# Seven block products for eight in an input projection, with the block sums on GpSimd

## What is computed

```python
h = modulated rmsnorm of x                    # (2304, 1024)
parts = split(h @ w_in)                       # w_in (1024, 4096): q, k, v, gate of four head groups
A: window attention   B: neighbourhood attention   C: retention   D: HGRN2 (bounds from the forget columns)
mixed = concat(out_A * silu(gate_A), ..., out_D * silu(gate_D))
x = x + gate_mod * rmsnorm(mixed @ w_out)     # w_out (1024, 1024)
```

## Time and profile before

| | |
|---|---|
| time, median of 3 runs | 3869.07 us (3867.66 to 3869.54) |
| span of the profiled execution | 3870.5 us |
| TensorE busy | 3759.0 us, 97% |
| TensorE weight loads | 2057.6 us, 53% (beside matmuls) |
| VectorE, ScalarE, GpSimd busy | 2311.2, 1186.4, 515.0 us |
| HBM traffic | 386.67 MB, 100 GB/s |
| stages of layer 0 on TensorE | first 43 to 343 us, win to 767, nei to 1202, rest to 1560, HGRN and output to 1961 |

### The profile page before, as it was taken

One profiled execution on the slowest core, in us unless ns is written; L12 is line 12 of the kernel. 1 busy time (PEld: TensorE's weight loads), 2 busy tenths in 40 slices (PEclk: granted clock), 3 DMA queues, 4 the chain that ended last, 5 costly groups with the idle time before them and its releaser, 6 DMA issues.

```text
span 3870.5 us, 62967 instructions
## 1 busy us (share of the span) xinstructions
PE 3759.0 (97%) x24449; PEld 2057.6 (53%) x24449; DVE 2311.2 (60%) x4739; ACT 1186.4 (31%) x3257; POOL 515.0 (13%) x798
## 2 busy tenths in 40 slices
PE   7999999999999998899999999999999999989998
PEld 4544555545554455555544445554555545555554
DVE  2334345323667978999932333552246688889996
ACT  3311223223332122344442023222333311224443
POOL 2100000100000155100000000001000003540000
PEclk9999999999999999899999999999999999979999
DMA  7443121132222434332432031213222233352322
GB/s 249 139 140 103 50 72 53 61 105 69 88 88 86 130 104 129 134 124 99 145 120 90 38 102 50 69 48 115 70 82 73 74 119 115 117 165 96 123 100 85
DMA packets 234360, 388.87 MB, mean 100 GB/s; under 512 B 30001, under 2 KB 150033, under 8 KB 233937
## 3 DMA queue, kind: packets, MB, share of 16 engines
q1 hardware_dynamic: 194096, 262.55, 21.9%
q0 software_dynamic: 39968, 122.30, 8.3%
HBM read 264.42 MB, written 122.25 MB: 100 GB/s over the span
## 4 chain that ended last, share of the span: by engine, by line
PE 91%; DVE 5%; SPq 1%; DMA 1%; issue 1%; ACT 1%; POOL 0%; DVEq 0%; ACTq 0%; POOLq 0%
PE ps L1170 51%; PE ps L1524 13%; PE ps L1307 6%; PE ps L1289 4%; PE ps L1276 3%; PE ps L1280 2%; PE ps L1477 2%; PE ps L1439 2%; PE ps L1349 1%; PE ps L1236 1%; PE ps L1418 1%; PE ps L1502 1%; DVE e_t L2077 1%; PE ps L1182 1%; PE ps L1506 1%
## 5 line engine op out<-in xcount | busy, mean ns | idle before, releaser
L1170 PE MATMUL ps<-w_sb,hT 128*128 128x512 f32 x4608 | 2174.0, 606 | 3.7 <-ACT hT L1671 2.4
L1170 PEld LDWEIGHTS ps<-w_sb,hT 128*128 128x128 f32 x4608 | 812.5, 190 | 772.6 <-issue 737.8
L1524 PE MATMUL ps<-wo_sb,mT 128*128 128x512 f32 x1152 | 534.5, 604 | 2.6 <-ACT mT L1841 2.6
L979 POOL DMA_DIRECT2D projected<-row_t x252 | 137.1, 544 | 2336.5 <-DVE row_t L2080 1084.8
L2077 DVE RECIPROCAL e_t<-e_t 128x256 f32<-128x256 f32 (+1 forms) x180 | 430.7, 2393 | 6.2
L1524 PEld LDWEIGHTS ps<-wo_sb,mT 128*128 128x128 f32 x1152 | 205.9, 190 | 206.6 <-issue 196.5
L2075 DVE TENSOR_SCALAR e_t<-e_t 128x256 f32<-128x256 f32 (+1 forms) x180 | 62.2, 346 | 207.9 <-ACT row_t L1689 186.3
L1683 ACT ACTIVATE row_t<-ps 128x512 f32<-128x512 f32 x108 | 64.5, 597 | 393.9 <-PE ps L1170 388.0
L2184 DVE TENSOR_REDUCE nei_st<-ps 128x2 f32<-128x512 f32 x72 | 49.7, 691 | 211.1 <-PE ps L1280 211.1
L2217 DVE COPY win_pT<-ps 128x512 f32<-128x512 f32 x64 | 44.2, 691 | 213.5 <-PE ps L1289 213.5
L2217 DVE COPY nei_pT<-ps 128x512 f32<-128x512 f32 x64 | 44.2, 691 | 207.8 <-PE ps L1289 207.8
(11 more groups left out here) (248 smaller groups left out, 5172.5 us busy)
## 6 DMA issues: line engine op xcount, KB each, us to landing
projected<-row_t POOLq DMA_DIRECT2D x288, 256.0 KB, 2.5
w_sb<-in_w_in SPq DMA_DIRECT2D x14, 2048.0 KB, 9.2
hg_raw<-projected SPq DMA_DIRECT2D x72, 256.0 KB, 3.9
...
hg_braw<-projected SPq DMA_DIRECT2D x108, 128.0 KB, 2.6
...
```

The source lines that it names most:

```text
L979: pool.dma_start(rows[tok(t), g * GRP:(g + 1) * GRP], row_t[:, p.slot]).then_inc(row_stored[p.slot], 16)
L1170: mm = nc.tensor.matmul(ps[:, p.bank, :], hT[:, k, t * P:(t + 1) * P], w_sb[:, g % 2, k, :], start=(k == 0), stop=(k == KC - 1))
L1524: mm = nc.tensor.matmul(ps[:, 6 + g, :], mT[:, t % 2, k, :], wo_sb[:, k, g * GRP:(g + 1) * GRP], start=(k == 0), stop=(k == KC - 1))
```

## The change

For groups 0 to 5 two neighbouring tiles (t0 = 2i, t1 = 2i + 1) and one group make a *unit*: a block product of a 2x2 block matrix (tiles by halves of the inner channels) with a 2x2 block matrix (`b11`, `b12`, `b21`, `b22`: 512 channels x 256 columns each). It is computed by seven block products in the order P1, P2, P6, P5, P7, P3, P4, each of 4 matmuls of 128x256. Four of them have token sums as the stationary operand: s1 = t1 upper + t1 lower half, s3 = t0 upper - t1 upper, s2 = s1 - t0 upper, s4 = t0 lower - s2. Four have weight sums as the moving one: t2 = b22 - b12 + b11 (two operations), t1 = b22 - t2, t3 = t2 - b11, t4 = b21 - t2, made once for a group. All of these sums are GpSimd's: 4 of 128x512 for a unit, 5 of 128x1024 for a group. P6 and P7 accumulate in PSUM on P1, P3 on P5, P4 on P7.

ScalarE copies P1, P6, P5 and P4 out of PSUM (`take_part`), VectorE adds a kept part to P2, P7 and P3 on the way out (`add_part`); product k waits until product k - 2 of its bank is out. SiLU is made by 256-column blocks from `row_t` (`silu_block`). GpSimd's order for a unit is `unit_sums`: s4, the next unit's s1, at a change of group t2 and t1 of the next, s3, s2, then t3 and t4, then the two stores. The weights come in four block loads of 0.5 MB, issued by ScalarE while the last unit of the group before runs (after P1 the upper two, after P6 the lower two); layer 0's first by SyncE. `fill` gives 14 small matmuls to a slot (2, 3, 4, 2, 3), and still 8 large ones where pieces are plain. `LEAD` is one unit. In the first stage `turn_x` stands after 7 of a slot's 14 matmuls and `normed`, `modulated` run one tile further ahead. The 38 band DMAs stand behind the sums and stores of unit 1. At the end of layer 0 GpSimd makes layer 1's first sums. `oml` is gone and some tiles and semaphores share a place; groups 6 and 7 stay as they were.

```diff
-ALL_PIECES = ([(g, t) for g in range(6) for t in range(NT)] + [(g, BACK[i]) for g in (6, 7) for i in (0, 1)]
-              + [(g, t) for t in BACK[2:] for g in (6, 7)])
-
-LEAD = 2
+UNIT_GROUPS = 6
+PAIRS = NT // 2
+UNITS = [(g, i) for g in range(UNIT_GROUPS) for i in range(PAIRS)]
+PLAIN = ([(g, BACK[i]) for g in (6, 7) for i in (0, 1)] + [(g, t) for t in BACK[2:] for g in (6, 7)])
+LEAD = 1
 
...
-AT_WIN, AT_NEI, AT_REST = 2 * NT, 4 * NT + LEAD, 6 * NT + 2 * LEAD
-PROJ_ORDER = {"first": ALL_PIECES[:AT_WIN], "win": ALL_PIECES[AT_WIN:AT_NEI], "nei": ALL_PIECES[AT_NEI:AT_REST], "rest": ALL_PIECES[AT_REST:]}
+AT_WIN, AT_NEI = 2 * PAIRS, 4 * PAIRS + LEAD
+PLAIN_NEI = 2 * (NT + AT_NEI + LEAD - len(UNITS))
+UNIT_ORDER = {"first": UNITS[:AT_WIN], "win": UNITS[AT_WIN:AT_NEI], "nei": UNITS[AT_NEI:]}
+PLAIN_ORDER = {"first": [], "win": [], "nei": PLAIN[:PLAIN_NEI], "rest": PLAIN[PLAIN_NEI:]}
+P1, P2, P6, P5, P7, P3, P4 = range(7)
+BY_ACT = {P1: 1, P6: 2, P5: 3, P4: 4}
+BY_DVE = {P2: 1, P7: 2, P3: 3}
+S1, S3, S2, S4 = range(1, 5)
+HB = GRP // 2
+KH = KC // 2
+def w_places(g):
+    c, d, spare = ((2, 3, 7), (7, 2, 3), (3, 7, 2))[g % 3]
+    return {"b11": 0, "b21": 1, "b12": c, "t2": c, "b22": d, "t1": 4, "t3": 5, "t4": 6, "spare": spare}
+BLOCKS = {"b11": (0, 0), "b12": (0, 1), "b21": (1, 0), "b22": (1, 1)}
...
+    def load_block(eng, l, g, name):
+        kh, nh = BLOCKS[name]
+        at = g * GRP + nh * HB
+        src = w_in[l, kh * KH * P:(kh + 1) * KH * P, at:at + HB].rearrange("(k p) n -> p k n", p=P)
+        eng.dma_start(w_blk[:, w_places(g)[name], :].rearrange("p (k n) -> p k n", n=HB), src).then_inc(lower_in if kh else upper_in, 16)
...
+            def make_s1(u):
+                t0, t1 = u.tiles
+                if u.g == 0:
+                    pool.wait_ge(h_act, u.l * NT + t1 + 1)
+                    pool.wait_ge(h_dve, u.l * NT + t1 + 1)
+                nc.gpsimd.tensor_tensor(s_t[:, 0], half(t1, 0), half(t1, 1), ALU.add).then_inc(s_made, 1)
+            def make_s3(u):
+                t0, t1 = u.tiles
+                nc.gpsimd.tensor_tensor(s_t[:, 2], half(t0, 0), half(t1, 0), ALU.subtract).then_inc(s_made, 1)
+            def make_s2(u):
+                pool.wait_ge(s_made, 4 * u.u + S1)
+                nc.gpsimd.tensor_tensor(s_t[:, 1], s_t[:, 0], half(u.tiles[0], 0), ALU.subtract).then_inc(s_made, 1)
+            def make_s4(u):
+                pool.wait_ge(s_made, 4 * u.u + S2)
+                nc.gpsimd.tensor_tensor(s_t[:, 1], half(u.tiles[0], 1), s_t[:, 1], ALU.subtract).then_inc(s_made, 1)
+            def make_t2(d, g):
+                at, n, made = w_places(g), d * UNIT_GROUPS + g, 5 * (d * UNIT_GROUPS + g)
+                for half_in in (upper_in, lower_in):
+                    pool.wait_ge(half_in, 32 * (n + 1))
+                t2 = w_blk[:, at["t2"], :]
+                nc.gpsimd.tensor_tensor(t2, w_blk[:, at["b22"], :], t2, ALU.subtract).then_inc(t_made, 1)
+                pool.wait_ge(t_made, made + 1)
+                nc.gpsimd.tensor_tensor(t2, t2, w_blk[:, at["b11"], :], ALU.add).then_inc(t_made, 1)
+                pool.wait_ge(t_made, made + 2)
...
+            def store_unit(u):
+                for k, t in enumerate(u.tiles):
+                    p = u.rows[k]
+                    if k == 0:
+                        pool.wait_ge(part_dve, 3 * u.u + BY_DVE[P3])
+                    else:
+                        pool.wait_ge(part_act, 4 * u.u + BY_ACT[P4])
+                        pool.wait_ge(part_dve, 3 * u.u + BY_DVE[P7])
+                    last = [n for key, n in u.block.items() if key[0] == k]
+                    if last:
+                        pool.wait_ge(blk_silu, max(last) + 1)
+                    pool.dma_start(rows[tok(t), u.g * GRP:(u.g + 1) * GRP], row_t[:, p.slot]).then_inc(row_stored[p.slot], 16)
+            def unit_sums(g, i, between=None):
+                u = UNIT[l, g, i]
+                n = UNITS.index((g, i)) + 1
+                after = UNIT[(l,) + UNITS[n]] if n < len(UNITS) else None
+                turn = after is not None and after.g != g
+                pool.wait_ge(proj_done, u.run + P6 + 1)
+                make_s4(u)
+                if after is not None:
+                    pool.wait_ge(proj_done, u.run + P5 + 1)
+                    make_s1(after)
+                if between is not None:
+                    store_out(between)
+                if turn:
+                    make_t2(l, g + 1)
+                    make_t1(l, g + 1)
+                if after is not None:
+                    pool.wait_ge(proj_done, u.run + P7 + 1)
+                    make_s3(after)
+                    pool.wait_ge(proj_done, u.run + P3 + 1)
+                    make_s2(after)
+                if turn:
+                    make_t3(l, g + 1)
+                    pool.wait_ge(proj_done, u.run + P4 + 1)
+                    make_t4(l, g + 1)
+                store_unit(u)
+            if l == 0:
+                make_t2(0, 0)
+                make_t1(0, 0)
+                make_t3(0, 0)
+                make_t4(0, 0)
+                first = UNIT[l, 0, 0]
+                make_s1(first)
+                make_s3(first)
+                make_s2(first)
+            for n, (g, i) in enumerate(UNIT_ORDER["first"]):
+                unit_sums(g, i)
+                if l == 0 and n == (MAKE_AT + 19) // 2:
+                    pool.wait_ge(setup, SETUP_DVE + DEC_DVE)
                     pool.dma_start(decays, dec_new[:, :, :]).then_inc(tables_out, 16)
-                if l == 0 and n == 2:
+                if l == 0 and n == 1:
...
+                    def product(k, x, w, opens=False):
+                        if u.run + k >= 2:
+                            before = RUN[u.run + k - 2]
+                            if before[1] is None:
+                                bank_out(pe, before[0])
+                            else:
+                                part_out(pe, *before)
+                        for c in range(KH):
+                            mm = nc.tensor.matmul(ps[:, (u.run + k) % 2, 0:HB], x[:, c], w_blk[:, at[w], c * HB:(c + 1) * HB],
+                                                  start=opens and c == 0, stop=(c == KH - 1), skip_group_check=not opens)
+                            if c == KH - 1:
+                                mm.then_inc(proj_done, 1)
+                            yield
+                    def own(t, kh):
+                        return hT[:, kh * KH:(kh + 1) * KH, t * P:(t + 1) * P]
+                    new = i == 0
...
+                    yield from product(P1, own(t0, 0), "b11", opens=True)
+                    if new:
+                        pe.wait_ge(lower_in, 32 * (u.group + 1))
+                    yield from product(P2, own(t0, 1), "b21", opens=True)
+                    if new:
+                        pe.wait_ge(t_made, 5 * u.group + 2)
+                    pe.wait_ge(s_made, 4 * u.u + S2)
+                    yield from product(P6, s_t[:, 1], "t2")
+                    if new:
+                        pe.wait_ge(t_made, 5 * u.group + 3)
+                    pe.wait_ge(s_made, 4 * u.u + S1)
+                    yield from product(P5, s_t[:, 0], "t1", opens=True)
+                    if new:
+                        pe.wait_ge(t_made, 5 * u.group + 4)
+                    pe.wait_ge(s_made, 4 * u.u + S3)
+                    yield from product(P7, s_t[:, 2], "t3")
+                    pe.wait_ge(s_made, 4 * u.u + S4)
+                    yield from product(P3, s_t[:, 1], "b22")
+                    if new:
+                        pe.wait_ge(t_made, 5 * u.group + 5)
+                    if g == 0:
+                        pe.wait_ge(h_act, l * NT + t1 + 1)
+                        pe.wait_ge(h_dve, l * NT + t1 + 1)
+                    yield from product(P4, own(t1, 1), "t4")
...
+                    woven = (2, 3, 4, 2, 3) if slot // 2 + LEAD < len(UNIT_ORDER[a.name]) else (1, 2, 2, 1, 2)
...
+            def take_part(g, i, k):
+                u = UNIT[l, g, i]
+                act.wait_ge(proj_done, u.run + k + 1)
+                bank = ps[:, (u.run + k) % 2, 0:HB]
+                if k == P1:
+                    need(act, part_dve, 3 * (u.u - 1) + BY_DVE[P7])
+                    out = p_t[:, 0]
+                elif k == P6:
+                    need(act, part_dve, 3 * (u.u - 1) + BY_DVE[P3])
+                    out = p_t[:, 1]
+                elif k == P5:
+                    act.wait_ge(part_dve, 3 * u.u + BY_DVE[P2])
+                    out = p_t[:, 0]
+                else:
+                    row_free(act, u.rows[1])
+                    out = row_t[:, u.rows[1].slot, 0:HB]
+                    if (1, 0) in u.block:
+                        blk_e(u.block[1, 0], bank)
+                nc.scalar.activation(out, bank, ACT.Copy).then_inc(part_act, 1)
+                if i == PAIRS - 1 and g + 1 < UNIT_GROUPS:
+                    if k == P1:
+                        load_block(act, l, g + 1, "b12")
```

(28 more changed lines are left out.)

437 lines of the change are left out of this document (277 added, 160 removed).

## The result

The changed kernel takes 3807.16 us (median of 4 runs, 3800.66 to 3810.65), the kernel before 3869.26 beside it: ratio 0.9833, 95% interval 0.9819 to 0.9847. Forecast were 3797 and 3740 to 3855. The profiled execution spans 3808.8 us, 61.7 less than before.

A forecast was written before the change was run, and what follows sets the result against it. TensorE, holding 91% of the chain, bounds the kernel. 184 us saved minus 112 lost (26 + 20 + 22 + 3 + 11 + 24 + 6) gains 72: 3798.5 us profiled, 3797 median; 8 in 10 for 3740 to 3855.

The forecast's parts named there:

- point 6: VectorE operations held off by GpSimd sums: 24 us lost at changes of group in win and nei, 6 elsewhere.
- Saved: Groups 0 to 5: 3024 matmuls of 0.43 us replace 1728 costing 1484 us, weight loads still hidden; 184 us saved.
- Point 1: Unit 2, once: GpSimd issues 38 band DMAs before s4, so P3 waits; 22.4 us plus half clock, 26 taken.
- Point 2: Groups 0 to 1, both layers: late blocks and weight sums delay P6 by 6.4 us, then P3; 20 us with clock.
- Point 3: Groups 1 to 2, both layers: the same lateness and two more DMA issues ahead of s4; 22 us.
- Point 4: Group 1 units of layer 1: late last SiLU block delays the store, then s4 before P3; 3 us.
- Point 5: Starts of the layers: P6 late in layer 0, `turn_x(2)` late by 2.9 us in layer 1; 11 us together.
- held until 11: Woven changes of group: `maxima` held until 11 us into the slot by gapless sums, 4.2 us lost, 5 with clock.
- in the programs the takes stand where the product ends: Emptying banks in groups 0 to 5: 0.6 of 1.72 us where the engine is free, leaving 1.1 us of cover.
- sums mostly in time: Rival, chance 0.23: blocks land in 4 us and VectorE slips between sums, so changes of group cost little; 3749 us.
- bound in the slots: Rival, chance 0.20: each of 72 woven units loses 0.8 us from silu, store and s4 before P3; 3855 us.
- load not hidden: Rival, chance 0.07: each product's first weight load shows, 83 us, 3880; if every load does, 4462.

The follow-up runs named there:

- experiment 1: Kernel before, each 128x512 projection matmul of groups 0 to 5 issued as two of 256 columns, no sums: 3886.37 us, ratio 1.0038.
- experiment 3: Changed kernel with ScalarE's part of layer 0's decay tables starting one position later: 3787.20 us, ratio 0.9779.
- experiment 4: Changed kernel with s3 and s2 made ahead of weight sums t2 and t1 in the last unit of groups 0 and 1: 3806.68 us, ratio 0.9831.
- Experiment 5: Changed kernel with GpSimd waiting for normalised tile 2 before weight sums t1, t3 and t4 at layer 1's start: 3800.61 us, ratio 0.9817.
- experiment 7: Changed kernel with weight sums cut to 32 of 1024 columns in every group but the first of a layer: 3773.61 us, ratio 0.9746.
- experiment 8: Changed kernel with each GpSimd sum issued as two instructions of half its columns: 3811.41 us, ratio 0.9841.
- experiment 6: Changed kernel with token sums cut to 4 of 128 columns in every unit but the first of a layer: 3760.24 us, ratio 0.9711.

## Why the prediction was right, and where it was not

The range and the sign held and the middle was 10 us low, but the sum came out near the truth partly by luck: point 6 was twice too high or more, and the decay tables, which I had not seen, cost about as much as it was too high.

- *Saved*, 184: 178.8 by the steps. The load stayed hidden, 0.2159 us a record. The rule of the Trainium skill (TensorE: Matmul & The Clock Gate, The mechanism), by which a load overlaps a matmul only where the row groups differ, is contradicted again, by loads of 0.19 us in steps of 0.216 in experiment 1; the same section also lets a load run ahead into a background weight buffer, and with that the steps agree. The 0.43 was too low by 0.0017 by the steps; experiment 1 leaves room for a little more, some 10 us where the steps have 7.6.
- *Point 1*, bands, 26: a wait of 25.2 us and 2.5 for the clock, where I had 22.4 and 3.4; removing it gave 20. Right in place and mechanism. The wait was 22.3 to 24.7 us in the traces of experiments 3, 4, 5, 7 and 8, whose edits do not move the band DMAs; in the changed kernel's GpSimd waited 7.67 us for neg_t, not 5.95.
- *Point 2*, groups 0 to 1: waits of 5.5 and 7.1 us, where I had 8.4 each. P6's 6.4 late is right; the second wait, of 2 us before P3, came in neither layer, because P6 and what follows ran at half clock behind the first, for 3.8 and 5.5 us (in layer 0 modulation matmuls of 1.9 us stand there too).
- *Point 3*, groups 1 to 2: 9.0 and 6.3 us of waits, 22 in the forecast with clock. The size is near, the step "the stage's barrier is covered by the wait" failed in layer 0: experiment 4 moved s2 and the wait grew. The condition that I had put behind it, that VectorE's last SiLU finds the port free, was the one that broke.
- *Point 4*, 3: one wait of 1.53 us in layer 1 and seven of 0.19, all before P3 and behind s4: 2.9 together. (My own 8.8 against 8.6 is 0.2 a unit, not the 0.3 that I then took.)
- *Point 5*, 11: in layer 0 P6 waited 2.5 us, and P1 1.6 more than before; together that is the 4 of the forecast, but P1's part was not in it. P1 began at 45.11 instead of 42.97, since a VectorE operation of 16 columns (L2332) took 1.77 us instead of 0.17 beside t2, so point 6's mechanism was at work here. In layer 1 `turn_x(2)` waited 7.53 where I had 2.9. I had placed `turn_x(2)` rightly, and left VectorE's three operations before it at their old durations though GpSimd's sums run beside them. Experiment 5 shows it.
- *Point 6*, held operations, 30: mis-sized, by the failed step "held until 11". At the six woven changes TensorE waited once for long, 3.63 us at groups 2 to 3 of layer 0, and that was for s2 and not for a held copy. Experiments 6 and 7 price all sums in win and nei at 9 and 6 us, 15 together, and both have that wait in them. Against the table's expected saving these stages lost nothing, and that is luck in part: TensorE's waits for the DMA of `nei_k_raw` fell from 8.8 to 1.5 us there, which I had not forecast and no run explains. A held operation waited mostly for the one sum that ran, up to 2.4 us: of 51 held SiLU tensor_scalars 43 passed no end of a sum. And at five of the six changes the blocks landed early: t2 began 14.1 to 15.1 us behind its unit's start, not 17, so half of the run lay ahead of the new unit. (At groups 2 to 3 of layer 0 they landed late, t2 began 20.2 us behind it, and there the one wait came.) Groups 3 to 4 of layer 0:

```profile
752.98 1.48 DVE L2378 TENSOR_SCALAR e_t<-e_t 128x256 f32<-128x256 f32 x1
...
758.67 0.72 DVE L2532 SCALAR_TENSOR_TENSOR win_st<-win_st,neg_sink 128x2 f32<-128x2 f32 x1
```
```profile
754.38 2.35 POOL L1072 TENSOR_TENSOR w_sb<-w_sb 128x1024 f32<-128x1024 f32 x1
...
758.10 1.27 POOL L1053 TENSOR_TENSOR s_t<-s_t,hT 128x512 f32<-128x512 f32 x1
759.33 2.35 POOL L1076 TENSOR_TENSOR w_sb<-w_sb 128x1024 f32<-128x1024 f32 x1
```

  The SiLU operation that began under t2's last sum ended at 754.46, 0.08 us into t1. The last of `maxima`, from 758.67, ended at 759.39, at the seam of s2 and t3, and not at 764. The row of 2.79 us on which I had built spans three sums whose seams have no gap, as I read it; it was one case, and experiment 8 has others that end at such a seam. The rule of the Trainium skill (SBUF — State Buffer, Who interferes with whom), a lock for a whole instruction, fits the 43 of 51 that left at the end of the sum that ran. It doesn't decide, since most of those sums had a gap behind them, where either reading frees VectorE; and the 102 of 214 seams at which a held operation was not released go beyond what it says.
- *Not in the forecast*: 15.0 us of waits behind the decay tables, 21 us by experiment 3. The step that failed is "in the programs the takes stand where the product ends". It holds for the takes, but ScalarE's generator stands between P5's and P4's, and I had not followed what that waits for. Before, a piece had a bank for 6.9 us, and ScalarE's waits of 2.7 to 3.3 us in the same generator cost TensorE nothing. Now a take has 1.72 us.

So the loss was 117 instead of 112, with 30 that became 15 or less, 15 to 21 that I had not seen, 5 more at layer 1's start, and more at half clock. The rival "sums mostly in time" had the woven changes right in the main (five of six) and the first stages wrong; "bound in the slots" and "load not hidden" are out, since no unit of win or nei has a regular wait and the step is 0.216.

What stays open: about half of the 15 us of experiment 1, why the waits for `nei_k_raw` fell, and why a seam without a gap releases VectorE one time and not another.
